# A bias added by DVE becomes a one-row matmul on PE, in the first stage of a three-layer forward pass

## The chip, the cores and the metric

The kernel runs on one core of a Trainium2 chip. The metric is the device time of one execution, in microseconds; a comparison uses the median of several executions.

## The reference

One hybrid layer (latent attention beside an RWKV-7 recurrence, then a mixture of 32 experts) is followed by two more layers of another design and a last norm, for 256 tokens of 1024 values, all in float32. The change touches the first projection stage, where the rates of the recurrence are made:

```python
h = rms_norm(x, g_mix)
proj = h @ w_in
feat = proj[..., MLA_IN:]                      # r, k, v, wl, al, gl
feat = feat + (prev - feat) * mu               # prev: the token before
w = -jax.nn.softplus(-(w0 + jnp.tanh(wl) @ w2)) - 0.5
a = jax.nn.sigmoid(a0 + al @ a2)
g = jax.nn.sigmoid(gl) @ g2
```

The vectors `w0` and `a0` have 512 values each and are added to every token's row before a sigmoid (the softplus and the exponentials behind `w` are later worked out from sigmoid(w0 + tanh(wl) @ w2)).

## The kernel before, in words

The kernel writes out the instruction stream of each engine by hand, stage by stage, with semaphores between the engines; a stage ends with a barrier of all engines. The first stage is `first_in`. It projects the normed input onto 2208 columns in nine tiles (`FIRST_TILES`): tile 0 is the lora part (`wl`, `al`, `gl`, 256 columns), tile 1 the 256 columns of `c_q`, tile 2 the 160 columns of `c_kv` and `k_rope`, tiles 3 to 8 are k, r and v, 256 columns each.

For each tile k, SP loads the float32 weights (1 MB) into one of two slots of `wt`; ACT makes the fp16 upper part (`high_part`, L242); DVE makes the fp16 rest (`low_part`, L249), which also frees the slot for the load after next; PE multiplies 48 times (`multiply`, L336); and ACT moves the product from PSUM to SBUF (`move`, L345). SP also sends, for each tile of `feat`, three transfers that shift it by one token into `prev` (`shift`, L1365). The loads on SP's queue stand in one order with these shifts.

Between the tiles each engine does side work, in an order fixed by the tile number k:

- DVE at k=1 mixes tile 0 with its shifted copy (`mix(0)`) and then raises `mixed`, which lets POOL issue the list `more`, and ACT go on with the squashing functions.
- PE at k=3 transposes the squashed lora part (L1672), ACT copies it to `loraT`, and PE does `lora(0)` for the first 128 tokens: two matmuls of 64 contraction rows and 512 columns each, one for `w` and one for `a` (L1646, L1647). They lie in different halves of the array's rows. Then PE transposes `c_kv` (L1679).
- DVE at k=3 adds the two bias rows to these PSUM results (`bias(0)`, L1552 and L1553), and ACT at k=4 applies the sigmoid in place (`lora_rates(0)`, L1416 and L1417), after `high_part` of tile 5 and ahead of its copy of `ckvT`.
- PE at k=4 waits for `biased` 1, does `lora(1)`, waits for `ckvT` (`ckv_out`) and makes the first queries (`queries(0)`, L1653). DVE at k=4 first makes the rotation tables and then does `bias(1)`; ACT at k=5 does `lora_rates(1)`.
- PE at k=5 makes `queries(1)`, waits for `biased` 2, and multiplies for `g` (L1691).

POOL issues the smaller loads on its own queue: `early`, the lora part of `mu`, the list `rows` (lora weights, `g_cq`, `g_ckv`, `w_uq`), the list `biases` (`w0` and `a0`, each spread over 128 partitions, 256 KB written each), then waits for `mixed` and issues `more` (up to 768 KB each, 1.5 MB in all), and after the fifth product the list `rest`, with the constants of later stages, `counting` (128x256, 128 KB) among them. The right half of `counting` holds ones.

The PSUM tile `sc` (named `in_pT` in the profile) has four banks of 512 columns; `lora(0)` writes banks 2 and 3, `lora(1)` banks 1 and 2.

Of the kernel before, what the change touches and what calls it, by code (L numbers as in the profile page):

```python
# [9 lines left out]
ALU = mybir.AluOpType  # L10
ACT = mybir.ActivationFunctionType
# [6 lines left out]
P = 128  # L18
# [141 lines left out]
def cols(vector):  # L160

    return vector.rearrange("(p c) -> p c", p=P)


def cols_of(vector):

    return vector.rearrange("(p c) -> p c", c=1)


def spread(vector):  # L170

    return vector.rearrange("(a n) -> a n", a=1).broadcast_to([P, vector.shape[0]])
# [1132 lines left out]
def first_in(nc, con, x, w, m, wt, tokens, shift_in, low, marks, positions, identity, late):  # L1305

    W0, A0, K_K = range(3)
# [3 lines left out]
    with ExitStack() as ctx:  # L1311
# [7 lines left out]
        loraT = sb("loraT", [P, TT, 2, P])  # L1319
# [5 lines left out]
        sc = pr.pT  # L1325
# [2 lines left out]
        heads = lambda ap, d: ap.rearrange("p t (h d) -> p t h d", d=d)  # L1328
        side = ["x0_in", "x1_in", "identity_in", "tile0_in", "tile1_in", "early_set", "squared", "kk_ready",
                "early_in", "mu_in", "rows_in", "more_in", "rest_in", "zeroed", "angles", "sines", "squashed", "mixed", "cq_turned",  # L1330
                "ckv_turned", "lora_turned", "cq_out", "ckv_out", "lora_out", "lora_done", "biases_in", "biased", "g_done",
                "g_out", "q_made", "q_out", "q_squared", "k_made", "v_made", "k_squared", "v_out", "qn_turned", "qn_out",
                "norms", "roots", "gains_ready", "vlink", "glink"] + [f"shift{j}" for j in shift_of]
        with Stage(nc, "in1", Projection.NAMES + side) as sems:
            pr.take(sems[:len(Projection.NAMES)])
            (x0_in, x1_in, identity_in, tile0_in, tile1_in, early_set, squared, kk_ready,
             early_in, mu_in, rows_in, more_in, rest_in, zeroed, angles, sines, squashed, mixed, cq_turned, ckv_turned, lora_turned,
             cq_out, ckv_out, lora_out, lora_done, biases_in, biased, g_done, g_out, q_made, q_out, q_squared, k_made, v_made,
             k_squared, v_out, qn_turned, qn_out, norms, roots, gains_ready, vlink, glink) = \
                sems[len(Projection.NAMES):len(Projection.NAMES) + len(side) - len(shift_of)]  # L1340
            pr.late = LateInputs((x0_in, x1_in), identity_in, (tile0_in, tile1_in), early_set, squared)
# [1 line left out]
            vectors = m.vectors(w)  # L1343
            early = [(pos_i[:], positions.rearrange("a (t p) -> p (a t)", p=P)), (gains[:, 0, :], spread(w["g_qn"])),
                     (gains[:, 1, :], spread(w["g_kn"])), late["inv_freq"]]
            mixing, lora_part = spread(w["rw_mu"]), 3 * RW_W
            rows = [(m.lora[0:64, 0, :], w["rw_w2"]), (m.lora[64:P, 0, :], w["rw_a2"]), (m.lora[:, 1, :], w["rw_g2"]),
                    (gcq[:], w["g_cq"].rearrange("(c p) -> p c", p=P)), (gckv[:], cols(w["g_ckv"])),
                    (m.uq, w["w_uq"].rearrange("(c p) h d -> p c (h d)", p=P))]
            biases = [(m.row[:, W0, :], spread(w["rw_w0"])), (m.row[:, A0, :], spread(w["rw_a0"]))]  # L1350
            more = [(m.mu[:, 0:lora_part], mixing[:, 0:lora_part]), (m.uk, w["w_uk"].rearrange("c h d -> c (h d)")),
                    (m.uv, w["w_uv"].rearrange("c h d -> c (h d)")), vectors[K_K]] + \
                   [(gn[lo:lo + 64, n:n + 1], cols_of(w[g][0:MLA_NOPE])) for lo in (0, 64) for n, g in enumerate(("g_qn", "g_kn"))]
            rest = [pair for n, pair in late.items() if n != "inv_freq"] + vectors[3:] + \
                   [(m.mla_gain, w["g_mla_out"].rearrange("(c p) -> p c", p=P))]

            with nc.Block(no_gpsimd_drain=True) as block:
# [26 lines left out]
                @block.gpsimd  # L1384
                def _(pool):
                    link = Link(pool, glink)
                    nc.gpsimd.memset(prev[0:1, 0, :], 0.0).then_inc(zeroed, 1)
                    pool.wait_ge(x1_in, 16)
                    for n, (into, source) in enumerate(early):
                        nc.gpsimd.dma_start(into, source, allow_slow_non_contiguous=n == 0).then_inc(early_in, 16)  # L1390
                    nc.gpsimd.dma_start(m.mu[:, lora_part:], mixing[:, lora_part:]).then_inc(mu_in, 16)
                    for into, source in rows:
                        nc.gpsimd.dma_start(into, source, allow_slow_non_contiguous=True).then_inc(rows_in, 16)
                    for into, source in biases:
                        nc.gpsimd.dma_start(into, source).then_inc(biases_in, 16)
                    pool.wait_ge(mixed, 1)
                    for into, source in more:
                        nc.gpsimd.dma_start(into, source, allow_slow_non_contiguous=True).then_inc(more_in, 16)
                    pool.wait_ge(pr.product, 5)
                    for into, source in rest:  # L1400
                        nc.gpsimd.dma_start(into, source, allow_slow_non_contiguous=True).then_inc(rest_in, 16)
                    pool.wait_ge(identity_in, 16)
                    pool.wait_ge(rest_in, 16 * len(rest))
                    link(nc.gpsimd.tensor_copy(low[:, 0, :], con["identity"]))
                    link(nc.gpsimd.tensor_copy(low[:, 1, :], con["diagonal"]))
                    link(nc.gpsimd.tensor_copy(marks[:, 0:P], con["identity"]))
                    link(nc.gpsimd.tensor_copy(marks[:, P:3 * P], con["counting"]))

                @block.scalar
                def _(act):  # L1410
                    copy = lambda into, source, **how: nc.scalar.activation(into, source, ACT.Copy, **how)

                    def lora_rates(t):

                        act.wait_ge(biased, t + 1)
                        nc.scalar.activation(m.sig[:, t, :], m.sig[:, t, :], ACT.Sigmoid)  # L1416
                        nc.scalar.activation(m.a[:, t, :], m.a[:, t, :], ACT.Sigmoid)  # L1417

                    def q_squares(t):

# [15 lines left out]
                    for k in range(n_tiles):  # L1436
# [54 lines left out]
                def _(dve):  # L1491
                    link = Link(dve, vlink)
                    v = nc.vector
# [51 lines left out]
                        v.tensor_tensor(into[:, own, :, 0:16], part[0], part[1], ALU.subtract)  # L1545
                        link(v.tensor_tensor(into[:, own, :, 16:32], part[2], part[3], ALU.add))

                    def bias(t):

                        dve.wait_ge(biases_in, 16 * len(biases))  # L1550
                        dve.wait_ge(lora_done, t + 1)
                        v.tensor_tensor(m.sig[:, t, :], sc[:, (2, 1)[t], :], m.row[:, W0, :], ALU.add)  # L1552
                        v.tensor_tensor(m.a[:, t, :], sc[:, (3, 2)[t], :], m.row[:, A0, :], ALU.add).then_inc(biased, 1)  # L1553

                    def query_norm(t):

                        dve.wait_ge(q_squared, t + 1)
                        link(v.tensor_reduce(nrm[:, 0, t, 0:MLA_H], sqq[:, t], AX_X, ALU.add))
                        rotate(heads(m.qr, MLA_ROPE), heads(m.qr, MLA_ROPE), 0, MLA_H, t, 1)
# [10 lines left out]
                    for k in range(n_tiles):  # L1570
# [15 lines left out]
                        if k == 3:  # L1586
                            dve.wait_ge(pr.moved, 3)
                            square_sum(z[:, 1, :], feat[:, :, Q_RANK:Q_RANK + KV_RANK])
                            square_sum(krsq[:], feat[:, :, Q_RANK + KV_RANK:MLA_IN])
                            ts(z[:, 0, :], z[:, 0, :], 1.0 / Q_RANK, EPS, ALU.mult, ALU.add)  # L1590
                            ts(z[:, 1, :], z[:, 1, :], 1.0 / KV_RANK, EPS, ALU.mult, ALU.add)
                            bias(0)
                        if k == 4:
                            dve.wait_ge(sines, 1)
                            rotation(0)
                            rotation(1)
                            rotate(heads(krr[:], MLA_ROPE), heads(feat[:, :, Q_RANK + KV_RANK:MLA_IN], MLA_ROPE), 1, 1)
                            bias(1)
                        if k == 5:
                            dve.wait_ge(more_in, 16 * len(more))  # L1600
                            mix(3)
# [37 lines left out]
                def _(pe):  # L1639
                    ident = con["identity"]  # L1640
                    T = nc.tensor

                    def lora(t):

                        pe.wait_ge(lora_out, 1)
                        T.matmul(sc[:, (2, 1)[t], :], loraT[0:64, t, 0, :], m.lora[0:64, 0, :], start=True, stop=True)  # L1646
                        T.matmul(sc[:, (3, 2)[t], :], loraT[64:P, t, 0, :], m.lora[64:P, 0, :], start=True, stop=True).then_inc(lora_done, 1)  # L1647

                    def queries(t):

# [7 lines left out]
                    for k in range(n_tiles):  # L1658
# [20 lines left out]
                                ins = T.transpose(sc[:, 0, t * P:(t + 1) * P], feat[:, t, Q_RANK:Q_RANK + KV_RANK], ident)  # L1679
                            ins.then_inc(ckv_turned, 1)  # L1680
                        if k == 4:
                            pe.wait_ge(biased, 1)
                            lora(1)
                            pe.wait_ge(ckv_out, 1)
                            queries(0)
                        if k == 5:
                            pe.wait_ge(q_out, 1)
                            queries(1)
                            pe.wait_ge(biased, 2)
                            for t in range(TT):  # L1690
                                ins = T.matmul(sc[:, 1 + t, :], loraT[:, t, 1, :], m.lora[:, 1, :], start=True, stop=True)  # L1691
                            ins.then_inc(g_done, 1)
# [10 lines left out]
                        if k == 7:  # L1703
                            pe.wait_ge(v_out, 1)
                            for u in range(PAIR_UNITS):
                                for t in range(TT):
                                    at = u % 2 * SEQ + t * P
# [2079 lines left out]
```

## Time and profile before

| | |
|---|---|
| median of three runs | 1124.7 us (1124.56, 1124.7, 1127.84) |
| the profiled execution | 1124.56 us |
| its span, first to last instruction | 1122.8 us |
| PE busy | 984.0 us (88% of the span) |
| DVE busy | 592.5 us (53%) |
| ACT busy | 486.0 us (43%) |
| POOL busy | 99.7 us (9%) |
| the first stage | 0 to about 82 us |

In the rows, PE is the matmul engine and PEld its weight load, DVE the vector engine, ACT the scalar engine, POOL and SP issue transfers here (POOLq, SPq). `out<-in` are the kernel's tiles: `ring` is one large buffer that holds most of the stage's tiles, so its name says little and the line has to be read. An fp32 matmul stands as two records. Brackets hold the idle time before an instruction and what ended it.

### The profile page before, as it was taken

The numbers are of one execution on the slowest core, as the hardware profiler recorded it, in microseconds if no ns is written. First come the engines' busy times: TensorE is split into PE (matmuls) and PEld (weight loads), VectorE is DVE, ScalarE is ACT, GpSimd is POOL, SyncE is SP. The second block draws the span as 40 slices with busy tenths as digits, with TensorE's granted clock in tenths as the row PEclk, the third lists the DMA queues.
The fourth block names the chain that finished last, engine by engine and source line by source line (L and its number), as shares of the span: only waits on it lengthen the run. The fifth ranks groups of instructions, "written<-read, shape, count | busy, mean of one in ns | idle before, by whom it ended". The sixth has DMA issues, their size and how long they took to land. (4 is left out here: it accounts for less than half of the span.)

```text
span 1122.8 us, 20158 instructions
## 1 busy us (share of the span) xinstructions
PE 984.0 (88%) x8491; PEld 701.2 (62%) x8491; DVE 592.5 (53%) x954; ACT 486.0 (43%) x795; POOL 99.7 (9%) x111
## 2 busy tenths in 40 slices
PE   6998899788666677998699999997998879999996
PEld 5676796553333335885448777765885536777773
DVE  5667787511000005688575545536657865645543
ACT  5556643210000014554555645525445656644532
POOL 3500630000000001052000000002040000000000
PEclk9999999699888899998799999998998999999998
DMA  9832017999999995542094665525421055666520
GB/s 276 275 91 78 2 41 315 420 406 421 421 420 421 421 403 157 170 131 76 31 344 133 205 224 193 183 72 154 151 83 76 1 211 183 225 224 218 185 82 38
DMA packets 108420, 229.08 MB, mean 204 GB/s; under 512 B 7113, under 2 KB 86011, under 8 KB 93755
## 3 DMA queue, kind: packets, MB, share of 16 engines
q1 hardware_dynamic: 105275, 219.38, 53.8%
q0 software_dynamic: 3072, 8.66, 2.7%
q8 instruction: 53, 0.87, 0.3%
q14 instruction: 20, 0.16, 0.0%
HBM read 225.15 MB, written 1.05 MB: 201 GB/s over the span
## 5 line engine op out<-in xcount | busy, mean ns | idle before, releaser
L524 DVE SCALAR_TENSOR_TENSOR ffn_wu_lo<-ffn_w_up,ffn_wu_hi 128x2048 f16<-128x2048 f32 x44 | 99.0, 2288 | 55.3 <-ACT ffn_wu_hi L449 55.3
L1132 PE MATMUL rw_pB<-ring,kept 128*32 128x256 f32 x864 | 71.2, 429 | 31.6 <-DMA ring<-in_w_up 21.1
L669 PE MATMUL ffn_pG<-ffn_hT_hi,ffn_wu_hi 128*128 128x256 f16 x352 | 95.9, 273 | 0.3
L669 PE MATMUL ffn_pG<-ffn_hT_hi,ffn_wu_lo 128*128 128x256 f16 x352 | 96.0, 273 | 0.0
L669 PE MATMUL ffn_pG<-ffn_hT_lo,ffn_wu_hi 128*128 128x256 f16 x352 | 95.9, 273 | 0.0
L669 PE MATMUL ffn_pU<-ffn_hT_hi,ffn_wu_hi 128*128 128x256 f16 x352 | 95.9, 273 | 0.0
L669 PE MATMUL ffn_pU<-ffn_hT_hi,ffn_wu_lo 128*128 128x256 f16 x352 | 95.9, 273 | 0.0
L669 PE MATMUL ffn_pU<-ffn_hT_lo,ffn_wu_hi 128*128 128x256 f16 x352 | 95.9, 273 | 0.0
L449 ACT ACTIVATE ffn_wu_hi<-ffn_w_up 128x2048 f16<-128x2048 f32 x44 | 81.7, 1901 | 2.4 <-DMA ffn_w_up<-in_ffn_w_gate 2.3
L1132 PEld LDWEIGHTS rw_pB<-ring,kept 128*32 128x32 f32 x864 | 38.8, 123 | 61.3 <-issue 48.6
L249 DVE SCALAR_TENSOR_TENSOR in_w_lo<-wt,in_w_hi 128x2048 f16<-128x2048 f32 (+2 forms) x22 | 52.4, 2380 | 36.3 <-ACT in_w_hi L242 35.9
L1065 DVE TENSOR_TENSOR rw_mu_a<-rw_pB,rw_mu_a 128x256 f32<-128x256 f32 x8 | 3.4, 424 | 127.9 <-PE rw_pB L1132 127.9
L542 DVE SCALAR_TENSOR_TENSOR ffn_hidden<-ffn_pU,ffn_gated 128x512 f32<-128x512 f32 x22 | 15.2, 691 | 90.4 <-ACT ffn_gated L463 90.4
L524 DVE SCALAR_TENSOR_TENSOR ffn_wd_lo<-ffn_w_down,ffn_wd_hi 128x2048 f16<-128x2048 f32 x22 | 50.4, 2292 | 22.1 <-ACT ffn_wd_hi L449 22.1
L678 PE MATMUL ffn_pY<-ffn_wd_hi,ffn_h_hi 128*128 128x512 f16 x176 | 53.6, 379 | 0.7 <-DVE ffn_h_lo L524 0.7
L678 PE MATMUL ffn_pY<-ffn_wd_hi,ffn_h_lo 128*128 128x512 f16 x176 | 53.7, 379 | 0.0
L678 PE MATMUL ffn_pY<-ffn_wd_lo,ffn_h_hi 128*128 128x512 f16 x176 | 53.6, 379 | 0.0
L463 ACT ACTIVATE ffn_gated<-ffn_pG 128x512 f32<-128x512 f32 x22 | 13.1, 597 | 93.2 <-PE ffn_pU L669 93.0
L336 PE MATMUL in_pY<-in_w_hi,in_sT_hi 128*128 128x256 f16 (+2 forms) x352 | 45.1, 277 | 1.3 <-ACT in_sT_hi L275 0.3
L242 ACT ACTIVATE in_w_hi<-wt 128x2048 f16<-128x2048 f32 (+2 forms) x22 | 42.2, 1917 | 4.8 <-DMA wt<-in_od_w_in 2.8
L336 PE MATMUL in_pY<-in_w_hi,in_sT_lo 128*128 128x256 f16 (+2 forms) x352 | 43.2, 277 | 0.0
L336 PE MATMUL in_pY<-in_w_lo,in_sT_hi 128*128 128x256 f16 (+2 forms) x352 | 42.2, 273 | 0.0
(653 smaller groups left out, 2096.6 us busy)
## 6 DMA issues: line engine op xcount, KB each, us to landing
ring<-in_w_gate SPq DMA_DIRECT2D x27, 1024.0 KB, 26.1
ring<-in_w_up SPq DMA_DIRECT2D x27, 1024.0 KB, 26.4
ring<-in_w_down SPq DMA_DIRECT2D x26, 1024.0 KB, 26.5
ffn_w_up<-in_ffn_w_gate SPq DMA_DIRECT2D x22, 1024.0 KB, 7.7
ffn_w_up<-in_ffn_w_up SPq DMA_DIRECT2D x22, 1024.0 KB, 9.9
ffn_w_down<-in_ffn_w_down SPq DMA_DIRECT2D x22, 1024.0 KB, 5.1
wt<-in_ev_w_in SPq DMA_DIRECT2D x9, 1024.0 KB, 5.7
wt<-in_od_w_in SPq DMA_DIRECT2D x9, 1024.0 KB, 5.6
```

The lines of the kernel that those rows point to most:

```text
L242: self.nc.scalar.activation(self.w_hi[:, k % 2, :, 0:n], self.wt[:, k % 2, :, 0:n], ACT.Copy, scale=W_SCALE).then_inc(self.hi_ready, 1)
L249: self.nc.vector.scalar_tensor_tensor(self.w_lo[:, k % 2, :, 0:n], self.wt[:, k % 2, :, 0:n], W_SCALE, self.w_hi[:, k % 2, :, 0:n], ALU.mu ...
L336: ins = self.nc.tensor.matmul(self.pY[:, slot, t, 0:n], x[:, c, t * P:(t + 1) * P], w[:, slot, c, 0:n], start=(term == 0 and c == 0), stop ...
L449: copy = lambda o, i, scale=1.0: nc.scalar.activation(o, i, ACT.Copy, scale=scale)
L463: nc.scalar.activation(gated[:, s, :], pG[:, s, :], ACT.Silu, scale=1.0 / W_SCALE).then_inc(silu_done, 1)
L524: return nc.vector.scalar_tensor_tensor(out, whole, scale, hi, ALU.mult, ALU.subtract)
L542: nc.vector.scalar_tensor_tensor(into, pU[:, s, :], 1.0 / W_SCALE, gated[:, s, :], ALU.mult, ALU.mult).then_inc(hidden_ready, 1)
L669: ins = T.matmul(p[:, s, j * SEQ:(j + 1) * SEQ], w[:, s, m, c, j::NJ], h[:, c, :], start=(n == 0), stop=(n == 3 * KC - 1))
L678: return T.matmul(pY[:, t, half * 512:(half + 1) * 512], h[:, s, at:at + P], w[:, s, j, half * 512:(half + 1) * 512], start=False, stop=st ...
L1065: nc.vector.tensor_tensor(hidden[:], pU[:, 0:D_EXPERT], gated[:], ALU.mult).then_inc(hidden_ready, 1)
L1132: ins = nc.tensor.matmul(into[i * CAP:(i + 1) * CAP, 0:D_EXPERT], h[:, c, i * CAP:(i + 1) * CAP], held[:, c * D_EXPERT:(c + 1) * D_EXPERT] ...
```

## The change

The addition of `w0` and `a0` leaves DVE. `lora(t)` on PE first multiplies a row of ones (one partition of `counting`) with the bias row, 512 columns, into each of the two banks, and the two lora matmuls then accumulate onto it. The bias matmuls are issued ahead of the wait for `loraT`. ACT reads the sums straight from PSUM, and its two sigmoids raise `sig_ready` and `a_ready`, for which PE waits where it waited for `biased`. The bias vectors are loaded into one partition only, and `counting` moves from `rest` to `rows`.

```diff
             rows = [(m.lora[0:64, 0, :], w["rw_w2"]), (m.lora[64:P, 0, :], w["rw_a2"]), (m.lora[:, 1, :], w["rw_g2"]),
+                    late["counting"], (m.row[0:1, W0, :], one_row(w["rw_w0"])), (m.row[0:1, A0, :], one_row(w["rw_a0"])),
                     (gcq[:], w["g_cq"].rearrange("(c p) -> p c", p=P)), (gckv[:], cols(w["g_ckv"])),
                     (m.uq, w["w_uq"].rearrange("(c p) h d -> p c (h d)", p=P))]
-            biases = [(m.row[:, W0, :], spread(w["rw_w0"])), (m.row[:, A0, :], spread(w["rw_a0"]))]
...
-                    for into, source in biases:
-                        nc.gpsimd.dma_start(into, source).then_inc(biases_in, 16)
...
-                        act.wait_ge(biased, t + 1)
-                        nc.scalar.activation(m.sig[:, t, :], m.sig[:, t, :], ACT.Sigmoid)
-                        nc.scalar.activation(m.a[:, t, :], m.a[:, t, :], ACT.Sigmoid)
+                        act.wait_ge(lora_done, t + 1)
+                        at = (2, 1)[t]
+                        nc.scalar.activation(m.sig[:, t, :], sc[:, at, :], ACT.Sigmoid).then_inc(sig_ready, 1)
+                        nc.scalar.activation(m.a[:, t, :], sc[:, (3, 2)[t], :], ACT.Sigmoid).then_inc(a_ready, 1)
...
-                    def bias(t):
-
-                        dve.wait_ge(biases_in, 16 * len(biases))
-                        dve.wait_ge(lora_done, t + 1)
-                        v.tensor_tensor(m.sig[:, t, :], sc[:, (2, 1)[t], :], m.row[:, W0, :], ALU.add)
-                        v.tensor_tensor(m.a[:, t, :], sc[:, (3, 2)[t], :], m.row[:, A0, :], ALU.add).then_inc(biased, 1)
...
                     def lora(t):
 
+                        for which, bank in ((W0, (2, 1)[t]), (A0, (3, 2)[t])):
+                            T.matmul(sc[:, bank, :], con["counting"][0:1, P:2 * P], m.row[0:1, which, :], start=True, stop=False,
+                                     skip_group_check=True)
                         pe.wait_ge(lora_out, 1)
-                        T.matmul(sc[:, (2, 1)[t], :], loraT[0:64, t, 0, :], m.lora[0:64, 0, :], start=True, stop=True)
-                        T.matmul(sc[:, (3, 2)[t], :], loraT[64:P, t, 0, :], m.lora[64:P, 0, :], start=True, stop=True).then_inc(lora_done, 1)
+                        T.matmul(sc[:, (2, 1)[t], :], loraT[0:64, t, 0, :], m.lora[0:64, 0, :], start=False, stop=True,
+                                 skip_group_check=True)
+                        T.matmul(sc[:, (3, 2)[t], :], loraT[64:P, t, 0, :], m.lora[64:P, 0, :], start=False, stop=True,
+                                 skip_group_check=True).then_inc(lora_done, 1)
...
                         if k == 4:
-                            pe.wait_ge(biased, 1)
+                            pe.wait_ge(sig_ready, 1)
+                            pe.wait_ge(a_ready, 1)
                             lora(1)
...
-                            pe.wait_ge(biased, 2)
+                            pe.wait_ge(sig_ready, 2)
+                            pe.wait_ge(a_ready, 2)
                             for t in range(TT):
                                 ins = T.matmul(sc[:, 1 + t, :], loraT[:, t, 1, :], m.lora[:, 1, :], start=True, stop=True)
```

## Rows read from the trace of the kernel before

**Rows 1.** The page: the span, and the granted clock of PE by slice.
```profile
span 1122.8 us, 20158 instructions
...
PEclk9999999699888899998799999998998999999998
```

**Rows 2.** The longest wait of PE, 12 to 80 us: total, times, longest.
```profile
PE in_pT L1653 <- ACT ring L1411: 1.6, 1, 1.6
```

**Rows 3.** Stretches: PE, PEld, DVE, ACT, POOL busy; clock; DMA share; GB/s.
```profile
45.30:77.70 32.40, 32.38 (x229) 24.93 (x230) 25.48 (x56) 18.89 (x32) 10.21 (x19) 1.00 0.56 163
34.80:45.30 10.50, 7.97 (x58) 5.45 (x58) 6.05 (x14) 6.22 (x8) 2.31 (x5) 1.00 0.88 260
12.20:34.80 22.60, 22.14 (x202) 18.19 (x200) 16.34 (x33) 13.07 (x20) 5.78 (x11) 1.00 0.88 270
```

**Rows 4.** Timeline of PE, 34 to 48.2 us: start, us, engine, line, operation.
```profile
35.57 0.66 PE L1646 MATMUL in_pT<-ring,fi_loraT 64*128 64x512 f32 x1 [0.78 <-ACT fi_loraT L1411]
...
36.63 0.44 PE L1679 MATMUL in_pT<-con_identity,ring 128*128 128x128 f32 x2
37.27 1.92 PE L336 MATMUL in_pY<-ring 128*128 128x256 f16 x16 [0.21 <-ACT ring L242]
...
42.62 0.69 PE L1646 MATMUL in_pT<-ring,fi_loraT 64*128 64x512 f32 x1
...
45.33 2.85 PE L1653 MATMUL in_pT<-ring 128*128 128x384 f32 x8 [1.58 <-ACT ring L1411]
```

**Rows 5.** Timeline of ACT, 29 to 46 us.
```profile
34.82 0.60 ACT L1411 ACTIVATE fi_loraT<-in_pT 128x512 f32<-128x512 f32 x1 [3.74 <-PE in_pT L1672]
...
41.96 1.91 ACT L242 ACTIVATE ring<-wt 128x2048 f16<-128x2048 f32 x1 [4.26 <-DMA wt<-in_w_in]
...
44.30 0.61 ACT L1417 ACTIVATE rw_mu_a<-rw_mu_a 128x512 f32<-128x512 f32 x1
44.82 0.46 ACT L1411 ACTIVATE ring<-in_pT,fi_gckv 128x256 f32<-128x256 f32 x1
```

**Rows 6.** Timeline of PE: fp32 matmuls of 512 and 128 columns, and what follows.
```profile
55.83 1.88 PE L1691 MATMUL in_pT<-ring,fi_loraT 128*128 128x512 f32 x4
57.55 0.71 PE L336 MATMUL in_pY<-ring 128*128 128x256 f16 x5
...
90.25 0.92 PE L2028 MATMUL rw_pB<-kept 32*128 32x128 f32 x8
91.11 0.39 PE L2018 MATMUL rw_pB<-low 128*128 128x256 bf16 x2
```

**Rows 7.** Timeline of DVE and ACT, 47 to 54 us.
```profile
48.77 0.69 DVE L1552 TENSOR_TENSOR ring<-in_pT,ring 128x512 f32<-128x512 f32 x1
...
50.10 0.63 ACT L1416 ACTIVATE ring<-ring 128x512 f32<-128x512 f32 x1 [2.54 <-DVE rw_mu_a L1553]
...
53.45 0.60 ACT L345 ACTIVATE ring<-in_pY 128x512 f32<-128x512 f32 x1 [1.32 <-PE in_pY L336]
```

**Rows 8.** DMA: queue shares, 32 to 36.4 us; issues of tiles 3, 4.
```profile
q0 software_dynamic: 331, 1.30, 97.6%
q1 hardware_dynamic: 6, 0.01, 0.4%
...
wt<-in_w_in SPq DMA_DIRECT2D x1, 1024.0 KB, 6.7
...
wt<-in_w_in SPq DMA_DIRECT2D x1, 1024.0 KB, 5.6
```

**Rows 9.** Timeline of DVE and SP, 26 to 39 us.
```profile
27.19 0.69 DVE L1494 TENSOR_TENSOR ring<-ring 128x512 f32<-128x512 f32 x1 [2.46 <-DMA ring<-ring]
...
31.79 0.58 SPq L1380 DMA_DIRECT2D wt<-in_w_in  x1
```

**Rows 10.** Timeline, 77 to 83 us: the last result tile, the next stage.
```profile
77.78 0.60 ACT L345 ACTIVATE ring<-in_pY 128x512 f32<-128x512 f32 x1 [1.80 <-PE in_pY L336]
...
82.18 1.22 DVE L2518 TENSOR_REDUCE rw_st<-ring 128x16 f32<-128x1024 f32 x1 [3.23 <-PEq L157]
```

More of the change, by code:

```diff
@@ L1330, in first_in @@
                 "early_in", "mu_in", "rows_in", "more_in", "rest_in", "zeroed", "angles", "sines", "squashed", "mixed", "cq_turned",
-                "ckv_turned", "lora_turned", "cq_out", "ckv_out", "lora_out", "lora_done", "biases_in", "biased", "g_done",
+                "ckv_turned", "lora_turned", "cq_out", "ckv_out", "lora_out", "lora_done", "sig_ready", "a_ready", "g_done",
                 "g_out", "q_made", "q_out", "q_squared", "k_made", "v_made", "k_squared", "v_out", "qn_turned", "qn_out",
@@ L1337, in first_in @@
              early_in, mu_in, rows_in, more_in, rest_in, zeroed, angles, sines, squashed, mixed, cq_turned, ckv_turned, lora_turned,
-             cq_out, ckv_out, lora_out, lora_done, biases_in, biased, g_done, g_out, q_made, q_out, q_squared, k_made, v_made,
+             cq_out, ckv_out, lora_out, lora_done, sig_ready, a_ready, g_done, g_out, q_made, q_out, q_squared, k_made, v_made,
              k_squared, v_out, qn_turned, qn_out, norms, roots, gains_ready, vlink, glink) = \
@@ L1345, in first_in @@
                      (gains[:, 1, :], spread(w["g_kn"])), late["inv_freq"]]
+            one_row = lambda v: v.rearrange("(a n) -> a n", a=1)
             mixing, lora_part = spread(w["rw_mu"]), 3 * RW_W
             rows = [(m.lora[0:64, 0, :], w["rw_w2"]), (m.lora[64:P, 0, :], w["rw_a2"]), (m.lora[:, 1, :], w["rw_g2"]),
+                    late["counting"], (m.row[0:1, W0, :], one_row(w["rw_w0"])), (m.row[0:1, A0, :], one_row(w["rw_a0"])),
                     (gcq[:], w["g_cq"].rearrange("(c p) -> p c", p=P)), (gckv[:], cols(w["g_ckv"])),
                     (m.uq, w["w_uq"].rearrange("(c p) h d -> p c (h d)", p=P))]
-            biases = [(m.row[:, W0, :], spread(w["rw_w0"])), (m.row[:, A0, :], spread(w["rw_a0"]))]
             more = [(m.mu[:, 0:lora_part], mixing[:, 0:lora_part]), (m.uk, w["w_uk"].rearrange("c h d -> c (h d)")),
@@ L1353, in first_in @@
                    [(gn[lo:lo + 64, n:n + 1], cols_of(w[g][0:MLA_NOPE])) for lo in (0, 64) for n, g in enumerate(("g_qn", "g_kn"))]
-            rest = [pair for n, pair in late.items() if n != "inv_freq"] + vectors[3:] + \
+            rest = [pair for n, pair in late.items() if n not in ("inv_freq", "counting")] + vectors[3:] + \
                    [(m.mla_gain, w["g_mla_out"].rearrange("(c p) -> p c", p=P))]
@@ L1591, in _ @@
                             ts(z[:, 1, :], z[:, 1, :], 1.0 / KV_RANK, EPS, ALU.mult, ALU.add)
-                            bias(0)
                         if k == 4:
@@ L1597, in _ @@
                             rotate(heads(krr[:], MLA_ROPE), heads(feat[:, :, Q_RANK + KV_RANK:MLA_IN], MLA_ROPE), 1, 1)
-                            bias(1)
                         if k == 5:
```

## The prediction

> **What bounds the kernel now.** I read the page first, then the waits of PE, then the timeline of the first stage, which is the only part the diff touches. The profiled execution took 1124.56 us, of which its span is 1122.8 us [rows 1]; the median of the three runs shown is 1124.7, so 0.1 us more. I make the sum against 1124.56.
>
> The first stage ends at about 82 us. Between 12 and 34.8 us PE is busy 22.14 of 22.60 us, and between 45.3 and 77.7 us 32.38 of 32.40 us, at a granted clock of 1.00 [rows 3]. Between them it is busy 7.97 of 10.50, at the same clock; its longest wait in the stage, 1.6 us, is for ACT's copy of `ckvT` [rows 2], and 0.78 us more goes to waiting for the copy of `loraT` [rows 4]. After PE's last product the move starts at 77.78, SP sends the three shift transfers behind it, and the next stage starts at 82.18, all engines together behind a barrier [rows 10]. So whatever moves PE at 45.33 moves the start of the next stage, and what moves DVE or ACT alone does not.
>
> The wait that ends at 45.33 [rows 4] is read on ACT [rows 5]: it idles 4.26 us until weight tile 5 has landed, at 41.96, splits it, does the two sigmoids (the second is 44.30 to 44.91), and only then copies `ckvT` (44.82 to 45.28), which PE wants. PE had been through with `lora(1)` since about 43.75, and was idle 1.58 us. That idle time is cover, but only for work whose inputs are there before 45.3.
>
> **The change, part by part.**
>
> *Removed from DVE:* four PSUM additions, 0.69 us each (one is shown in [rows 7]), 2.7 us. None is waited for on the way to 45.33. The second pair is what ACT waits for, 2.54 us, before `lora_rates(1)`; but ACT idles another 1.32 us for PE's product straight afterwards [rows 7], and PE has no wait there [rows 3]. So the 2.54 us turn into a longer wait for PE: worth 0. If that cover were not there they would be worth up to 2.5 us (a rival below). ACT's sigmoids now read PSUM: the copy of 512 columns from PSUM is 0.60 us, the sigmoid of 512 from SBUF 0.61 [rows 5]; no change.
>
> *Added to PE:* in each `lora(t)` two fp32 matmuls with one row of weights against 512 columns. No matmul with one contraction row is in the trace. From above: two fp32 matmuls of 128 rows and 512 columns (four records, L1691) take from 55.83 to the next start at 57.55, so 0.86 us each. A second bound: four 32-row matmuls of 128 columns (L2028) take 90.25 to 91.11, so 0.215 each, and four times that is 0.86 again [rows 6]. From 128 rows down to 32 the price goes with columns alone, so I take 0.86, 1.72 for the pair; the bound below is nothing. Both bias rows lie in partition 0, in the row group that L1646 also uses, so they can't run side by side as L1646 and L1647 do (1.06 us for both, 35.57 to 36.63) [rows 4].
>
> The extra change of tile shape costs no more than a tenth here: the 32-row group in [rows 6] starts and ends on schedule between two other shapes. The Trainium skill (TensorEngine Tiling (Array Packing), Key Properties) says a change of tiling mode drains the array, which speaks against this change; it gives no time, so by it the sum would only be "+2.1 us or more", and these rows show no such gap.
>
> *Moved: who frees PE for `lora(1)`.* Before, PE waited for `biased` 1, which DVE gave before PE arrived: PE is not idle ahead of 42.62 [rows 4]. After, it waits for `sig_ready` and `a_ready`, which ACT gives after both sigmoids, and these stand behind tile 5: 44.91 [rows 5]. So `lora(1)`, which had used the idle time, is pushed out of it. Behind the waiting PE stand `queries(0)`, the whole product of tile 5 and everything to 77.7. Worked out: 44.91 plus 0.05 for the reaction (the copy's end at 45.28 to PE's start at 45.33, [rows 4, 5]) is 44.96; two bias matmuls, 46.68; the lora pair 1.06, 47.74; `queries(0)` starts there and not at 45.33: **+2.4 us**.
>
> *`lora(0)`:* its bias matmuls go out before the wait for `loraT`, so 0.78 us of them is covered [rows 4]. The pair ends at 34.8 + 1.72 = 36.5, the lora pair at 37.6, the two transposes (0.44) at 38.0, so tile 4's product starts 0.75 later than 37.27. It then ends at 43.4, still before 44.96: hidden, with 1.6 us in hand. Without that cover it would be +0.75.
>
> *DMA:* two loads of 256 KB go; two of 2 KB and `counting` (128 KB, from `rest`) go ahead of the MLA inputs. That is 380 KB (0.39 MB) less before 20 us, or 1.4 us at the 270 GB/s of 12.2 to 34.8 us [rows 3]. POOL issues one transfer more there and one fewer later, while it has nothing else to do. What can it reach? DVE waits until 27.19 for the shift transfers of tile 0 [rows 9], which queue behind tile 3; `mix(0)` then leads, one to one, to the split of tile 3, the load of tile 5 (31.79) and to `mixed`, which releases `more`. Tile 3 took 6.7 us to land, tile 4, alone, 5.6 [rows 8]; so the relief at 41.96 lies between 0 and 1.1 us. Tile 3's own issue waits for DVE and not for DMA, and most of the relief ends in tile 2, for which nothing on PE waits; I take 0.3.
>
> Tile 5 itself is no better off: it needs 10.1 us because its packets have 0.4% of the DMA time between 32 and 36.4 us while the POOL queue's `more` has 97.6% [rows 8]. The Trainium skill (DMA: Bandwidth & Descriptors, Queues, rings and completion order) has each DMA engine take turns between the queues with work, packet by packet. By that rule the early relief would be shared out as it comes and reach tile 5 with nothing, which makes the sum +2.4 instead of +2.1; the trace does not agree with turns in that stretch, and both sums lie in the forecast's own range.
>
> *Sum:* 0 + 0 + 2.4 − 0.3 = +2.1 us at 45.33, passed on whole through the dense stretch and the barrier: 1124.56 + 2.1 = **1126.7 us**.
>
> **Rivals.**
> 1. *The relief reaches tile 5 in full.* 1.1 us: +1.3, 1125.9. More than 1.6 can't be used, since PE arrives only at 43.4: floor +0.8. For it: DMA is 88% busy [rows 3]. Against: tile 3's issue.
> 2. *One-row matmuls cost next to nothing.* `lora(1)` then ends at 44.96 + 1.06 = 46.02 (+0.7), and with all the relief 1.1 earlier: −0.4, so 1124.2 to 1125.3. It passes zero when the bias pair costs less than 0.4 us and the relief is whole. Against: [rows 6].
> 3. *The other side: ACT's wait was on the path.* If removing the 2.54 us before `lora_rates(1)` counted, and the bias matmuls did not: 1124.56 − 2.5 = 1122.0. It decides only if ACT's 1.32 us of waiting for PE and PE's 0.02 us of idle time after 45.3 are misread.
> 4. *The longer gap costs clock.* PE now idles to 44.96. The page has slices at 0.8 later on [rows 1]; if the clock fell to the 1.2 GHz level after the gap, the 5.35 us product of a tile (37.27 to 42.62, [rows 4]) would take 10.7: +5.4 more, 1132. Against: the gap before was 1.58 us and the clock stayed at 1.00 [rows 3]; the new one, 43.4 to 44.96, is as long.
> 5. *The bias rows come late.* They are on the POOL queue ahead of inputs whose wait PE and ACT pass without idle time before; the two rows are 2 KB each, and by rows 3 even 128 KB are 0.5 us. I see no price for it.
>
> **How the numbers follow.** Forecast 0.66 (its own range 1126.1 to 1127.3). Rival 1: 0.14. Rival 2: 0.07. Rival 3: 0.04. Rivals 4 and 5, and re-timing of the later DMA-bound stretch: 0.09. One of the three runs before stood at 1127.84, 3 us above the others, so the median may carry some of that. The range that leaves out 2 in 10 at most is 1124.4 to 1128.3. A difference of 0.3% is 3.4 us, about what this kernel's measurement can tell from none: faster by that (below 1121.3) has no mechanism but part of rival 3, 0.03; slower (above 1128.1) is rivals 4 and 5 and the scatter, 0.12; the same, 0.85.
>
> **What would show it.** In the changed profile: no DVE additions at L1552; PE idle after tile 4's product until ACT's second sigmoid, near 44.7, then four records with one row of weights, 0.43 us apart, and `queries(0)` at 47.4 and not 45.3; tile 4's product from 38.0; ACT's wait before the second sigmoids nearly gone and its wait for PE's product grown from 1.3 to about 4; PE without a gap from there, and the next stage 2.1 us later. I am wrong if the one-row records are much shorter than 0.43, if tile 5 lands before 41, if PE shows new gaps after 48, or if the later stages differ in length by more than a microsecond.

## The result, and the profile after

The changed kernel takes 1141.2 us (median of four; 1132.8 to 1151.8) beside 1126.1 us (1124.6 to 1127.8) for the kernel before in the same comparison: a ratio of 1.0109, with a 95% interval of 1.0066 to 1.0152. The forecast was 1126.7 us. The change makes the kernel slower: by 1.1% here, and by 0.7% over all executions, as follows. Here and below a ratio leaves out the executions that took over 1.5% more than the fastest of their kernel, so it is not the quotient of the two medians.

Four runs of each are few, because both kernels scatter. Over all comparisons below, the kernel before was executed 119 times: 1122.5 to 1143.1 us, mean 1130.7 (standard error 0.5). The changed kernel was executed 60 times: 1130.0 to 1151.8, mean 1138.2 (0.6). So the change costs 7.6 us, with a standard error of 0.8, and not the 15 us that the first medians show. Those four runs of the kernel before all lay near the lower end of its spread.

The page of the profile after; the second row is the granted clock of PE in 40 slices of 28 us.

```profile
span 1135.1 us, 20168 instructions
...
PEclk9899899799888898998889999998998999999999
```

Beside [rows 1] the first half has more slices at 8: time at the 1.2 GHz level now appears in the second and the fifth slice (28 to 57 and 114 to 142 us), where the kernel before had none. The same, closer, in stretches of the first stage ("stage 1" below; the stage that follows it, up to about 430 us, is the second). The columns are those of [rows 3]; the clock is the third number from the right.

```profile
34.70:37.80 3.10, 3.10 (x10) 1.09 (x10) 0.56 (x1) 2.88 (x3) 0.00 (x0) 1.00 0.79 221
37.80:41.20 3.40, 3.40 (x17) 2.48 (x18) 2.81 (x11) 0.00 (x0) 0.00 (x0) 0.50 0.98 296
41.20:48.00 6.80, 6.46 (x43) 4.13 (x41) 3.44 (x8) 3.73 (x5) 2.68 (x6) 1.00 0.71 220
48.00:51.40 3.40, 3.40 (x7) 1.66 (x6) 2.24 (x9) 2.88 (x3) 3.40 (x7) 0.50 0.95 275
51.40:82.30 30.90, 30.90 (x226) 24.01 (x225) 20.11 (x39) 15.60 (x28) 7.70 (x11) 1.00 0.43 132
```

The clock is 0.50, the 1.2 GHz level, twice for 3.4 us. Both times PE had no idle time in the stretch, and both times it had just done the one-row matmuls and `lora(t)`. The first fall had no wait of PE ahead of it: the only wait that the view of PE's waits lists for stage 1 stands later, ahead of `lora(1)` (total, times, longest).

```profile
PE in_pT L1637 <- ACT rw_mu_a L1417: 0.3, 1, 0.3
```

PE's timeline after, beside [rows 4]:

```profile
34.71 1.98 PE L1637 MATMUL in_pT<-ring,con_counting 1*128 1x512 f32 x4
36.62 0.69 PE L1640 MATMUL in_pT<-ring,fi_loraT 64*128 64x512 f32 x1
...
37.68 0.64 PE L1675 MATMUL in_pT<-con_identity,ring 128*128 128x128 f32 x2
38.11 3.42 PE L336 MATMUL in_pY<-ring 128*128 128x256 f16 x16
41.37 1.91 PE L336 MATMUL in_pY<-ring,kept 128*128 128x256 f16 x16
...
45.37 1.95 PE L1637 MATMUL in_pT<-ring,con_counting 1*128 1x512 f32 x4 [0.34 <-ACT rw_mu_a L1417]
47.25 0.69 PE L1640 MATMUL in_pT<-ring,fi_loraT 64*128 64x512 f32 x1
...
48.53 3.95 PE L1649 MATMUL in_pT<-ring 128*128 128x384 f32 x7
```

The first third of tile 4's product takes 3.42 us here, from 38.11, against 1.92 in [rows 4]. `queries(0)` starts at 48.53 instead of 45.33. ACT's timeline after, beside [rows 5] and [rows 7]:

```profile
42.34 1.91 ACT L242 ACTIVATE ring<-wt 128x2048 f16<-128x2048 f32 x1 [4.64 <-DMA wt<-in_w_in]
...
44.63 0.59 ACT L1417 ACTIVATE rw_mu_a<-in_pT 128x512 f32<-128x512 f32 x1
...
50.04 0.58 ACT L1416 ACTIVATE ring<-in_pT 128x512 f32<-128x512 f32 x1
...
52.84 1.00 ACT L1410 ACTIVATE ring<-in_pT 128x256 f32<-128x256 f32 x4 [1.74 <-PE in_pT L1649]
```

Tile 5 lands at 42.34 (41.96 before). ACT's wait of 2.54 us before `lora_rates(1)` is gone. And the end of the stage, beside [rows 10]:

```profile
82.41 0.60 ACT L345 ACTIVATE ring<-in_pY 128x512 f32<-128x512 f32 x1 [1.80 <-PE in_pY L336]
...
86.81 1.22 DVE L2516 TENSOR_REDUCE rw_st<-ring 128x16 f32<-128x1024 f32 x1 [3.24 <-PEq L157]
```

The next stage starts 4.6 us later than in [rows 10]. In four traces of the changed kernel it starts at 86.8, 88.3, 88.0 and 88.2 us, in three of the kernel before at 82.2, 81.5 and 82.2: 5.9 us more in the mean.

### The profile page after: what moved, and what is told of

Its sections match the earlier page's. It is cut to its first block and busy times, and to the rows that moved or that the text cites. A ratio compares the mean times of both kernels' runs of the same rounds, so it can differ in the third digit from the quotient of the medians.

```text
span 1135.1 us, 20168 instructions
## 1 busy us (share of the span) xinstructions
PE 998.4 (88%) x8497; PEld 710.3 (63%) x8499; DVE 590.4 (52%) x950; ACT 486.3 (43%) x795; POOL 101.3 (9%) x111
## 5 line engine op out<-in xcount | busy, mean ns | idle before, releaser
L1153 PE MATMUL rw_pB<-ring,rw_mu_a 128*32 128x512 f32 x240 | 34.4, 679 | 11.2 <-DMA ring<-in_w_down 7.9
```

The source lines that it names most:

```text
L1153: ins = nc.tensor.matmul(pD[i * CAP:(i + 1) * CAP, half, :], hidT[:, j, i * CAP:(i + 1) * CAP], held[:, at:at + 512], start=(j == 0), stop ...
```

## The experiments

They came in five groups on one chip each. "Before" is the kernel before, run among them; ratios are to it, with 95% intervals.

**Group 1: four first cuts.** `full_rows` is the changed kernel with bias matmuls of 128 rows; its weights are the identity and each bias is again spread over 128 partitions (so the 256 KB loads are back). The matmul's side of the edit:

```diff
-  T.matmul(sc[:, bank, :], con["counting"][0:1, P:2 * P], m.row[0:1, which, :], start=True, stop=False,
+  T.matmul(sc[:, bank, :], ident, m.row[:, which, :], start=True, stop=False,
...
```

> The changed kernel with the bias matmuls on all 128 rows: the identity as weights and the bias spread over 128 partitions; same count, columns and waits, result the same. Theory A (one-row matmuls bring the clock down): the first stage stays at the full clock, queries(0) starts near 47.4 to 47.8 us and not at 48.5, the next stage at 84.5 and not at 86.7, and the median is about 1128. Theory B (the gap and the order of waits do it, whatever the rows): two drops of 3.4 us in the first stage as in the changed kernel, next stage at 86.7, median near 1140.

`no_bias_mm` is the changed kernel without the four bias matmuls, so that `w0` and `a0` are left out of both rates.

> The changed kernel without the four bias matmuls (the bias is left out of both rates). What is left is the new wait of PE for ACT's sigmoids. Theory A: queries(0) starts 1.1 to 1.3 us later than in the kernel before (lora(1) after the second sigmoid, near 46.4 to 46.6), clock at full in the first stage, median 1126 to 1127. Theory B: the clock still falls behind the gap of PE near 42.6 to 45 us, and the median is over 1130.

`before_one_row` is the kernel before with two one-row fp32 matmuls of 512 columns ahead of each `lora` pair, whose results are overwritten.

```diff
+  for bank in ((2, 1)[t], (3, 2)[t]):
+      T.matmul(sc[:, bank, :], ident[0:1, :], m.lora[0:1, 0, :], start=True, stop=True)
   pe.wait_ge(lora_out, 1)
```

> The kernel before, bias still on DVE, with two fp32 matmuls of one row and 512 columns added ahead of each pair of lora matmuls, whose banks are overwritten afterwards. Theory A: the clock falls in the first stage behind them, as in the changed kernel; the first pair delays tile 4 by 0.8 us, the second pair takes 1.6 of idle time before ckvT; the median is over 1130 if these drops do the damage. Theory B (waits): no drop, at most 1 us more, 1125 to 1127.

`before_late` is the kernel before with 35 filler matmuls at the end of the first stage instead of 11, so that everything behind it comes later with nothing else changed.

> The kernel before with 35 instead of 11 of the dense filler matmuls that close the first stage: nothing else, so that the second stage starts about 4.6 us later, at 86.7, at full clock so far. Theory C (the drops of the second stage come only because it starts at another moment): drops of some 13 us appear between 100 and 125 us and the median is 1135 to 1142. Rival (they follow from the drops of the first stage or from the changed work): no drop before 205 us, median 1129 to 1130.

Measured, with before at 1130.5 (median of 35 executions): `full_rows` 1132.0, 1.0017 [0.9989, 1.0046]; `no_bias_mm` 1134.0, 1.0043 [1.0014, 1.0073]; `before_one_row` 1133.4, 1.0033 [0.9995, 1.0071]; `before_late` 1136.9, 1.0046 [1.0009, 1.0083]. The same bias on 128 rows, with the same waits, costs little, and neither half of the change alone reaches 7.6 us. That the new wait costs something without the bias matmuls is the reading of `no_bias_mm` alone; `full_rows`, which has the same wait, does not show it.

The medians expected above were set against 1124.7 us for the kernel before, which has 1130.5 here, so they have to be read as differences. By them `full_rows` (+1.4) is as theory A had it, `no_bias_mm` (+3.4) lies between the two, and `before_late` (+6.4) lies nearer its rival in time, though its trace has the low clock where theory C had it. What theory A said of the traces failed: `full_rows` had low clock in stage 1 in two of three traces (its first: `queries(0)` at 49.91, the next stage at 86.8), and `before_one_row` had none. Where the clock fell, in each trace:

| kernel (time of the traced executions) | next stage starts | PE idle near 44 us | low clock in stage 1 | low clock, 85 to 200 us |
|---|---|---|---|---|
| before, three traces (1123.7 to 1124.6) | 81.5 to 82.2 | 1.6, 1.3, 1.7 us | none | none |
| after, four traces (about 1137, 1143.0, 1135.6, 1131.1) | 86.8 to 88.3 | 0.3, 1.6, 1.5, 2.0 us | 6.8, 6.8, 6.8, 3.4 us | 13.7, 13.7, 6.8, 10.2 us |
| `full_rows`, three traces (1136.1, 1135.6, 1128.0) | 86.1 to 87.9 | 2.1, 2.4, 2.3 us | 3.4, 3.4, 0 us | 13.7, 6.8, 3.4 us |
| `no_bias_mm` (1141.4) | 84.4 | 2.3 | 3.4 | 23.9 |
| `before_one_row` (1131.0) | 84.4 | none | none | 13.7 |
| `before_late` (1144.1) | 89.8, with the filler | 2.0 | 3.4 | 30.7 |

The three executions of the kernel before that were traced are among its fastest, 6 us below its mean, and most of the others are not; so the table says more of what can happen than of how often.

So a part of the time lies behind the first stage, in code that the change does not touch. `before_late` shows that such falls also appear when that code is only moved in time; but it had one in stage 1 too, ahead of its edit, as the kernel before had not. Later groups show them in kernels with no such shift, so `before_late` does not settle why they come.

**Group 2: the order on ACT.** Does the wait that ends at `queries(0)` matter, and does it matter together with the one row? `after_again` repeats the changed kernel. `after_act_first` lets ACT do `lora_rates(0)` and the copy of `ckvT` before it waits for tile 5, `full_act_first` does the same to `full_rows`, and `before_ckv_first` moves only the copy of `ckvT` in the kernel before.

```diff
+  if k == 4:
+      lora_rates(0)
+      act.wait_ge(ckv_turned, 1)
+      copy(m.ckvT, sc[:, 0, 0:SEQ], scale=gckv[:, 0:1]).then_inc(ckv_out, 1)
   if 1 <= k < n_tiles - 1:
       pr.high_part(act, k + 1)
...
-  if k == 4:
-      lora_rates(0)
-      act.wait_ge(ckv_turned, 1)
-      copy(m.ckvT, sc[:, 0, 0:SEQ], scale=gckv[:, 0:1]).then_inc(ckv_out, 1)
```

> The changed kernel as it is, beside the kernel before on the same chip, since the kernel before by itself has spread over 1122.5 to 1143 us in 35 runs, the long ones with more time at the low clock. Theory A (one-row matmuls bring the clock down more often than the same matmuls on 128 rows): median 6 us or more over that of full_rows, which was 1132.0, and its fastest run over 1129. Theory D (the first result came from scatter between executions): median within 3 us of full_rows and of the kernel before plus 2.5 us.

> The changed kernel with ACT's work of step 4 in another order: sigmoids for the first tokens and the ckvT copy ahead of the split of tile 5, so that they use the 4 us in which ACT waits for tile 5. PE should no longer be idle between 43 and 45 us; queries(0) starts right behind lora(1), near 46. If the wait is the whole loss in the first stage, the median is 2 us or more below the changed kernel. If the one-row matmuls bring the clock down by themselves, a drop remains behind them in the first stage and the median stays above 1132.

> The same order of ACT, and the bias matmuls on all 128 rows (identity and spread bias). Theory A: no drop in the first stage, next stage at 83 to 84 us, and a median at or below that of the kernel before on this chip. Rival: drops come in the second stage regardless, and the median is within 2 us of full_rows.

> The kernel before with one thing moved: ACT copies ckvT ahead of the split of tile 5. PE's idle 1.6 us at 43.7 go, the next stage starts 1.6 us earlier, at 80.5. If gaps of this length let the clock fall in part of the executions, the median falls by more than 1.6 us; if not, by 1.6 us or less.

Measured, with before at 1128.8 (31): `after_again` 1138.7, 1.0078 [1.0046, 1.0111]; `after_act_first` 1134.0, 1.0037 [1.0006, 1.0069]; `full_act_first` 1132.8, 1.0014 [0.9983, 1.0045]; `before_ckv_first` 1130.2, 1.0034 [0.9995, 1.0073]. `after_again` lies 6.7 us over `full_rows` of group 1, as theory A had it. With ACT's order changed, PE has no idle time ahead of `lora(1)`, there is no low clock in stage 1, and the next stage starts at 83.3 us (`after_act_first`) and 82.9 (`full_act_first`). PE's timeline of `after_act_first`:

```profile
43.48 1.98 PE L1637 MATMUL in_pT<-ring,con_counting 1*128 1x512 f32 x4
...
46.45 2.85 PE L1649 MATMUL in_pT<-ring 128*128 128x384 f32 x8
```

`queries(0)` starts at 46.45 instead of 48.53, and takes its full-clock 2.85 us. That is one trace, of an execution of 1127.9 us, near the fastest of that kernel; its median of 1134.0 lies 4.7 us below `after_again`, as expected if the wait costs, and stays above the 1132 named beforehand for the case that the one row costs clock by itself. So this run decides neither way. `full_act_first` had 13.7 us of low clock in the second stage, as its rival had it. The kernel before gains nothing from losing its own gap (its next stage started at 81.5, and not at the 80.5 expected).

**Group 3: the dose.** If the one row is what costs clock, four times as much of it must show it. Both kernels are the kernel before with eight fp32 matmuls of 512 columns ahead of `lora(0)`; they differ only in the rows, and each has one of the two lines shown.

```diff
+  if t == 0:
+      for bank in (2, 3) * 4:
+          T.matmul(sc[:, bank, :], ident[0:1, :], m.lora[0:1, 0, :], start=True, stop=True)   # one_row_x4
+          T.matmul(sc[:, bank, :], ident[0:P, :], m.lora[0:P, 0, :], start=True, stop=True)   # full_rows_x4
```

> The kernel before, bias on DVE, with eight fp32 matmuls of one row and 512 columns ahead of the first pair of lora matmuls (their banks are overwritten afterwards), 6.9 us of them. Theory A (few rows bring the clock down): the granted clock falls to the lower level during or right behind them, near 36 to 44 us, with no gap on PE before it, and the first stage is over 7 us longer than its sum. Theory B (only gaps do it): clock full there, the stage longer by about 6 us.

> The same eight matmuls on all 128 rows. Theory A: clock full behind them, the first stage about 6 us longer than before and shorter than that of one_row_x4 by 1.7 us or more. Theory B: the same as one_row_x4, within 0.5 us.

> The changed kernel once more, beside full_rows on one chip, for another profile and for the comparison of one row with 128 rows. Theory A: median 4 us or more over full_rows_again, and drops in the first stage between 36 and 52 us. Theory B (rows don't matter): medians within 3 us.

> The changed kernel with the bias matmuls on 128 rows once more, for the same comparison. Theory A: a drop at most behind the gap near 43 to 45 us, none at 37 us; median 2 to 4 us over the kernel before. Theory B: as the changed kernel, 8 to 10 us over the kernel before.

Measured, with before at 1131.6 (29): `one_row_x4` 1146.2, 1.0143 [1.0093, 1.0193]; `full_rows_x4` 1131.7, 1.0006 [0.9970, 1.0042]; `after_third` 1135.0, 1.0050 [1.0015, 1.0086]; `full_rows_again` 1131.4, 1.0012 [0.9985, 1.0039]. PE's timeline and stretches of `one_row_x4`:

```profile
35.76 8.63 PE L1647 MATMUL in_pT<-ring,con_identity 1*128 1x512 f32 x16
44.32 1.22 PE L1649 MATMUL in_pT<-ring,fi_loraT 64*128 64x512 f32 x1
```

```profile
35.80:41.20 5.40, 5.40 (x14) 2.47 (x14) 2.88 (x8) 2.88 (x3) 0.00 (x0) 1.00 0.94 284
41.30:48.00 6.70, 6.70 (x16) 2.47 (x15) 1.84 (x7) 2.04 (x2) 0.00 (x0) 0.50 0.71 208
```

And of `full_rows_x4`:

```profile
34.49 7.03 PE L1647 MATMUL in_pT<-ring,con_identity 128*128 128x512 f32 x16
41.45 0.69 PE L1649 MATMUL in_pT<-ring,fi_loraT 64*128 64x512 f32 x1
```

```profile
34.50:41.40 6.90, 6.90 (x18) 2.84 (x16) 3.36 (x11) 2.88 (x3) 0.00 (x0) 1.00 0.81 228
41.50:48.10 6.60, 6.60 (x55) 5.12 (x54) 5.10 (x13) 3.42 (x4) 0.00 (x0) 1.00 0.66 195
```

PE is busy 6.70 of 6.70 us in the one and 6.60 of 6.60 in the other. With one row the clock falls to 0.50 while the sixteen records still run, which stretches them from 7.03 to 8.63 us, and stays there for 6.7 us. With 128 rows it stays at 1.00. The next stage starts at 90.7 us and at 86.0. The Trainium skill (TensorE: Matmul & The Clock Gate, Part 1) says that the clock follows how busy PE has been recently; these rows do not bear that out if busy means that a matmul is running.

Only 4.7 us of the difference between the two kernels lie in stage 1 of these traces. Both traces have 23.9 us of low clock in the second stage, and that of `full_rows_x4` is of its slowest execution (1147.7), so the traces do not place the rest. The clocks of all executions do: the mean time at the low level, worked out as in the last section, is 141 us with one row (6 executions) and 115 with 128 (12), and the mean times are 14.0 and 2.1 us over the kernel before. `one_row_x4` is as theory A had it (stage 1 longer by 8.7 us, over 7 expected). `after_third` lies 3.6 us over `full_rows_again`, where theory A wanted 4 or more and theory B less than 3, and `full_rows_again` lies at the kernel before, where 2 to 4 us more were expected.

**Group 4: single traces.** More traces of the three kernels, for the places of the falls: `before_p1` and `before_p2` are the kernel before, `after_p4` the changed one, `full_rows_p3` is `full_rows`.

> The kernel before, for its trace. If the additional low clock of the changed kernel lies in the first stage: no low clock or 3.4 us at most before 82 us here, and the second stage with low clock near 100 to 125 us in most executions as in the changed kernel. If it lies in the second: none between 85 and 200 us.

> The kernel before once more, for a third trace: no low clock or 3.4 us at most before 82 us, and low clock near 100 to 125 us, if the difference lies in the first stage; none from 85 to 200 us if it lies in the second.

> The changed kernel, for its trace: 6.8 us of low clock between 36 and 54 us for the fourth time, first stage 85 to 87 us, if it lies in the first stage; otherwise 0 to 3.4 us there.

> The changed kernel with bias matmuls on 128 rows, for its trace: 0 or 3.4 us of low clock in the first stage, behind the gap at 45 us and not at 38 us.

They took 1123.7, 1124.5, 1131.1 and 1128.0 us. The kernel before had no low clock up to 200 us in either, and `after_p4` had 3.4 us in stage 1 and not 6.8: both are what was expected if the additional low clock lies in the second stage. Stretches 36 to 54 us of `before_p1`:

```profile
36.00:54.00 18.00, 16.49 (x117) 12.26 (x116) 14.82 (x35) 10.27 (x16) 10.31 (x19) 1.00 0.90 267
```

of `after_again`:

```profile
36.00:54.00 18.00, 16.39 (x73) 8.89 (x72) 12.33 (x31) 8.64 (x10) 9.76 (x18) 0.81 0.87 256
```

and of `full_rows_p3`:

```profile
36.00:54.00 18.00, 15.69 (x93) 9.79 (x92) 11.67 (x30) 10.15 (x15) 9.71 (x18) 1.00 0.87 255
```

`before_p1` and `after_again` have PE busy equally long, 16.49 and 16.39 us. The number of matmuls done in that time (117 and 73) and the clock differ. `full_rows_p3` is the changed schedule with the clock at 1.00 throughout stage 1, and so the cleanest reading of what the forecast worked out. PE's timeline of it:

```profile
46.30 1.95 PE L1637 MATMUL in_pT<-ring,con_identity 128*128 128x512 f32 x4 [2.31 <-ACT rw_mu_a L1417]
...
49.25 2.85 PE L1649 MATMUL in_pT<-ring 128*128 128x384 f32 x8
```

Here tile 5 landed at 43.27, so `queries(0)` starts 5.98 us behind it. Before, it started 3.37 us behind it (45.33 − 41.96, [rows 4, 5]). The schedule itself costs 2.6 us, reckoned from the landing of tile 5.

**Group 5: a filled gap.** `fill_gap` is the kernel before with six dense fp16 matmuls of 512 columns, whose results are not used, behind `lora(1)`, where PE waits for `ckvT`. If the gap of 1.58 us cost clock later, filling it would gain.

```diff
   lora(1)
+  stream(T, sc[:, 3, :].rearrange("p (c s) -> p c s", s=SEQ), pr.sT_hi[:, 0, 0:P], pr.sT_hi[:, 0:2, :], 6)
   pe.wait_ge(ckv_out, 1)
```

> The kernel before with six dense fp16 matmuls of 512 columns (1.3 us, into a bank that is free) behind lora(1), where PE waits for ckvT. If that gap costs clock in many executions of the kernel before, the median falls by 2 us or more; if it does so seldom, the median is within 2 us of it; queries(0) starts at the same moment after tile 5 has landed, 3.4 us.

Measured: 1131.3 beside 1131.0 (17), 0.9992 [0.9957, 1.0026]. It gains nothing, and no version here beats the kernel before.

## Why the prediction was wrong

The forecast and the median of 1141.2 lie 14.6 us apart, in three parts. The kernel before was taken at 1124.56 us, and its mean over 119 executions is 1130.7: 6.1 us. The change was priced at 2.1 us and costs 7.6: 5.5 us. The median of the first four executions of the changed kernel lies 3.0 us over its mean of 60.

**The step that failed** is the price of the one-row matmuls under "Added to PE", together with the ground on which rival 4 was put aside. The step priced a matmul by its columns only. For the engine's time that price held: the pair took 1.91 us (34.71 to 36.62) where 1.72 was forecast, and 128 rows instead of one took 1.81 in `full_rows`. What it left out is the clock, a term that it put at nothing. Rival 4 named the falling clock as a risk of the gap, and was put aside because the gap was as long as before. It was (1.5 to 2.0 us in three of four traces), and the clock fell all the same. What the runs showed in its place is that the rows of the matmul count: eight one-row matmuls cost 14.7 us over the kernel before and eight 128-row ones 0.1 (medians), with PE busy throughout in both. The changed kernel itself was 6.2 us slower in the mean (standard error 0.9) than the same schedule with 128 rows (1138.2 over 60 executions, 1132.0 over 25 of `full_rows`), although that kernel loads more; on one chip, in group 3, it was 3.9 us (twelve executions of each).

What the gap adds is less clear.

| ratio to before, % | ACT late (as changed) | ACT first |
|---|---|---|
| one row | +0.78, +0.50 (first comparison +1.09) | +0.37 |
| 128 rows | +0.17, +0.12 | +0.14 |

The cells of the right column lie within each other's intervals, and so do those of group 3 in the left one; it is the executions taken together that part one row from 128. In the traces neither the one row nor a wait is needed for a fall in stage 1: the first fall of the changed kernel, at 37.8 us, and that of `one_row_x4` had no wait of PE ahead of them, and `full_rows`, `no_bias_mm` and `before_late` fell behind waits of 2.0 to 2.4 us with no one-row matmul. Where both came, at waits of 1.5 and 1.6 us, the low clock lasted 6.8 us; at waits of 1.3 to 1.7 us without one row there was none in three traces. That the two act together fits this and is not shown.

**What the 7.6 us are made of.** In the traces the next stage starts 5.9 us later. Of these 2.6 are the schedule, from `full_rows_p3`, and 0.8 are tile 5, which landed at 42.5 us in the mean of four traces and at 41.7 in that of three. The rest, 2.5, is what the low clock costs: about half of the 3.4 or 6.8 us at the low level, except that in the trace shown first the wait for ACT took up the first fall. The landing is scatter at least in part: `fill_gap`, `before_late` and `before_one_row`, with the loads of the kernel before, had it at 43.3 to 43.6.

That would leave 1.7 us for everything behind stage 1. But the split rests on three fast executions of the kernel before, and the means don't follow it: by the same reading stage 1 of `full_rows` is 5.0 us longer, and the whole kernel takes only 1.4 us more. The clock of every execution gives a better account of the whole. The mean time at the low level (the last section says how it is worked out) is 116 us for the kernel before, 126 for the changed one and 113 for `full_rows`. As an estimate, each microsecond of it costs between 0.3 us, as the executions of the changed kernel scatter, and 0.5, where PE never waits. With the schedule's 2.6 that makes 5.6 to 7.6 us for the changed kernel (7.6 measured) and 1.1 to 1.7 for `full_rows` (1.4 measured). So 3 to 5 of the 7.6 us are low clock. Of the 12.5 us more of it than in `full_rows`, 3.7 lie in stage 1 by the traces; so a part of the loss lies behind stage 1, in code that the change does not touch. For example, in the changed kernel:

```profile
102.60:106.10 3.50, 3.50 (x20) 2.36 (x16) 1.74 (x4) 1.60 (x8) 0.00 (x0) 0.51 0.00 0
112.90:123.10 10.20, 9.33 (x43) 9.18 (x44) 4.97 (x14) 1.69 (x3) 0.94 (x2) 0.50 0.01 2
```

`before_ckv_first` and `fill_gap`, whose times equal those of the kernel before, had 13.7 us there too, so the falls move from execution to execution. Why one-row matmuls at 35 to 47 us leave more low clock far behind them stays open.

**The other steps.**
- *Removed from DVE, worth 0:* as forecast. ACT's 2.54 us became a wait for PE (1.74 us at L1410), and nothing came sooner.
- *Moved, +2.4 us:* the mechanism was right and its size 2.6. PE is held until the second sigmoid and then does the bias pair: `no_bias_mm`, with the wait alone, had `queries(0)` 4.53 us behind tile 5 (46.39 − 41.86), 1.2 more than before. Of these 0.5 are low clock (its `lora` pair took 1.55 us and not 1.06), which leaves the 0.7 of rival 2; the bias pair adds the rest.
- *`lora(0)`, +0.75 hidden behind 1.6 us of idle time:* right at full clock: the product of tile 4 started at 38.11 (38.0 forecast). At low clock that cover is used up; PE then waited only 0.34 us ahead of `lora(1)`.
- *DMA relief, −0.3 us:* nothing arrived. Tile 5 landed at 42.34, 42.15, 41.85 and 43.70 after, against 41.96, 41.28 and 41.93 before. Tile 2 did land earlier (ACT's split at 20.7 to 21.9 instead of 21.9 to 22.5), and the relief ended there, because the issue of tile 3 waits for DVE.
- *Passed on whole, the later stages keeping their length:* right where the clock was alike. Behind stage 1 the kernel before took 1040.4 to 1040.6 us, `after_p4` 1041.1 (mean clock of the execution 0.958, before 0.953 to 0.956). The other three traces of the changed kernel took 1045.9 to 1052.9, at 0.939 to 0.945.
- *The range* took the scatter from three runs that lay within 3.3 us. The kernel's own scatter is 20 us, so a range of 4 us around any forecast was too narrow, and 0.3% is below what three runs can tell. Only 0.12 had been left for a time above 1128.1.

## What to carry to other kernels

A matmul that uses one row of the array costs the same time as a full one (within 0.1 us for a pair here), and it may also cost the clock of the work behind it; replacing a vector addition that nobody waits for by such a matmul has no gain to set against that. When work moves from an engine with slack to the engine that sets the end, list who now frees that engine: here a wait on ACT's sigmoids, behind a weight tile that landed late, pushed PE's work out of its idle time and cost 2.6 us. Before reading a difference of half a per cent, execute both kernels some thirty times (one execution of the kernel before scatters by 5 us, so the difference of two means of thirty has a standard error of 1.3, or 0.1%) and compare how long each ran at the lower clock.

## What the runs showed of the hardware

- The granted clock fell to the 1.2 GHz level with PE busy 6.70 of 6.70 us, in and behind one-row fp32 matmuls, and not in 128-row ones of the same length.
- The scatter of this single-core program is mostly time at low clock: over the executions of a kernel the time goes against the mean clock (correlation of 0.83 to 0.97 in size, kernel by kernel). An execution's span times twice what its mean clock lacks of 1 is its time at the lower level. Each microsecond of that goes with 0.35 us of time in the kernel before and 0.29 in the changed one. The means are 116 us (before, 115 executions with a clock on record), 126 (changed, 60) and 113 (`full_rows`, 25), with standard errors of 1 to 2 us.
- Tile 5, on SP's queue, again landed about 10 us after its issue, while the POOL queue had most of the DMA time. The queues' shares of the DMA time in the changed kernel, 32 to 37 us, beside [rows 8]:

```profile
q0 software_dynamic: 353, 1.45, 91.9%
q1 hardware_dynamic: 1, 0.00, 0.3%
```
